# Moving the gated product of a convolutional feed-forward network from VectorE to GpSimd

## The chip, the cores and the metric

One Trainium2 chip, one core of it in use. The metric is the device time of one execution in microseconds (us); lower is better. The engines in the text are PE (TensorE), ACT (ScalarE), DVE (VectorE), POOL (GpSimd) and SP (SyncE, which only issues transfers here).

## What is computed

A decoder trunk of two layers on 576 tokens (512 prompt positions and 8 sequences of 8 new positions) with 1024 features. Each layer is a mixer with three branches followed by a feed-forward network, both with a layer norm behind them. The part that matters here, cut from the reference:

```python
def conv_ffn(h, prefix, w_up, conv_w, conv_b, w_down):
    a = h @ w_up                                   # 1024 -> 2 x 2816
    ext = concatenate([prefix, a], axis=1)         # two earlier rows
    c = conv_b + conv_w[0] * ext[:, 0:T]
    for k in range(1, 3):
        c = c + conv_w[k] * ext[:, k:k + T]
    gate, up = split(c, 2, axis=-1)
    return (silu(gate) * up) @ w_down
```

The change touches the product `silu(gate) * up`, which is the input of the down projection.

## The kernel before

Everything is feature-major: a tile is 128 features by 576 tokens, and the matmuls take 288 tokens at a time. Each fp32 operand of a matmul is split in two parts, hi (fp32r, made by ACT, `weight_hi` and the `copy` at L542) and lo (the remainder, made by DVE, `weight_lo` and `lo` at L1399); a product takes three matmuls (hi times hi, weight hi times input lo, weight lo times input hi), all of them at L981.

The feed-forward network of a layer runs in two halves (`hf`) of 11 feature tiles (`FH`), so there are 44 **pairs** in the program. A pair `j` is a gate tile (par 0) and an up tile (par 1), each one a tile of PE with 8 x 6 matmuls into its own two PSUM banks. In the first half, the first three even pairs (`UP_FIRST = (0, 2, 4)`) are *halved*: tokens 0 to 287 of their tiles were multiplied earlier, beside the layer norm, and parked in `STASH`, so that PE has only 24 matmuls left for each tile. The text calls the other pairs full. After the 11 pairs come the down tiles.

What each engine does for a pair, in its own order:

- PE waits for the weights (`w_lo`) and for its PSUM banks (`mm_free`), and multiplies the two tiles.
- ACT (`up_tile`, L914 to L936), for par 0: wait for PE, copy the prefix and the PSUM banks to `EB` (this frees the banks), split the next weight (hi), wait for `c_ready`, Silu of the gate into `SL`. For par 1: the copies and the weight. Then it waits for `h_ready` and copies `HX` to `HH` (L936), and only then goes on to the next pair.
- DVE (`up_tile`, L1899 to L1943), for each par: three taps of the convolution (L1911, L1918, L1924) and two small copies to `TAIL`; par 0 ends with a drain that releases `c_ready`. The lo part of the weights for pair j+1: in a halved pair both stand within the convolutions, in a full pair the first stands behind par 0 and the second behind the product. Then the product: a drain, a wait for `silu`, two multiplications `SL * CC[1]` into `HX` (L1932 with 512 tokens, L1933 with the 64 sample tokens). Last, a wait for `h_hi` and the lo part of `HX` into `HL` (L1941, shown as L1399).
- POOL has nothing in this stage but the end of the layer norm before it: `norm(l, 2 * l, M_OUT)` ends with 16 additions of a bias (L488). Its next work is `norm(l, 2 * l + 1, M_DOWN[1])`, which begins with the last down tiles.
- SP fetches the weights, one tile ahead.

The first six pairs of the first half are written out, the rest run in loops (`Fori`) on ACT, DVE and PE; the last pair of each half stands behind its loop. The order across engines is set by counting semaphores: `n0`, the number of the pair, is the value that each of them is compared with.

```python
dve.drain()
dve.wait_ge(S["silu"], n0 + 1)
dve.tensor_tensor(HX[:, 0:SEQ], SL[:, 0:SEQ], CC[:, 1, 0:SEQ], ALU.mult)
dve.tensor_tensor(HX[:, SEQ:T]..., seqs(SL[:, CVP:CV], CVS)[:, :, 0:DS], ..., ALU.mult)\
    .then_inc(S["h_ready"], 1)
```

## Time and profile before

| what | value |
|---|---|
| median of 3 runs | 2149.49 us (2149.4 to 2158.35) |
| the profiled execution: its own time | 2150.36 us |
| its span | 2148.5 us |
| PE busy in the span | 2061.5 us, 96% |
| DVE busy | 1199.8 us, 56% |
| ACT busy | 800.5 us, 37% |
| POOL busy | 404.9 us, 19% |
| mean granted clock of PE | 0.986 of full speed |

Read it as a kernel in which PE is busy nearly all of the time, while the other engines feed it. All times of rows are counted from the start of the span. Layer 0 has its first up pairs from 651 us and its second half of pairs from about 848 us; layer 1 has the first up pairs from 1716 us.

### The profile page before, as it was taken

The page shows a single profiled execution, that of the slowest core. Times are in us where ns is not written, and L with a number is a line of the kernel's source. Part 1 is how long each engine was busy: PE and PEld are TensorE (multiplying, and loading weights), DVE is VectorE, ACT ScalarE, POOL GpSimd, SP SyncE. Part 2 cuts the span into 40 slices and gives each one's busy share as a digit, 9 for nine tenths or more (in the row PEclk, how much of TensorE's full clock was granted, in tenths as well). Part 3 has the DMA queues.
Part 4 walks back from the last instruction along what each step waited for, and adds up shares of the span by engine and source line. Part 5 has one row for each costly group of instructions (what it writes and reads, how often), then busy time and mean ns, then how long its engine had stood idle before and what let it go on. Part 6 is the DMA issues. An engine that isn't in the chain of part 4 may idle for free.

```text
span 2148.5 us, 42999 instructions
## 1 busy us (share of the span) xinstructions
PE 2061.5 (96%) x17374; PEld 1903.9 (89%) x17374; DVE 1199.8 (56%) x2036; ACT 800.5 (37%) x1502; POOL 404.9 (19%) x407
## 2 busy tenths in 40 slices
PE   8989999999998999999999899999999999999997
PEld 7976667999998999999989766679999889999997
DVE  4755445333578652666757554453335876436665
ACT  4333445222354331333443343342223543213334
POOL 0025662000051000000350266600001600000012
PEclk9989999999999999999999899999999999999999
DMA  7347996222433232225451499952225332222252
GB/s 259 107 147 283 367 366 248 77 87 79 154 108 98 81 103 66 79 87 175 137 198 64 137 354 364 362 191 88 78 84 167 95 103 78 98 64 87 78 192 72
DMA packets 88849, 325.68 MB, mean 152 GB/s; under 512 B 10576, under 2 KB 15568, under 8 KB 88592
## 3 DMA queue, kind: packets, MB, share of 16 engines
q1 hardware_dynamic: 46512, 169.51, 24.2%
q0 software_dynamic: 37440, 144.98, 18.1%
q10 hardware_dynamic: 4768, 9.37, 1.3%
q8 instruction: 92, 1.51, 0.3%
q14 instruction: 37, 0.30, 0.0%
HBM read 315.52 MB, written 7.26 MB: 150 GB/s over the span
## 4 chain that ended last, share of the span: by engine, by line
PE 84%; DVE 8%; ACT 3%; DMA 2%; issue 1%; DVEq 1%; POOL 0%; ACTq 0%; SPq 0%; POOLq 0%
PE PS L981 64%; PE PS L1229 5%; PE PS L1258 5%; DVE m_WL L1399 2%; PE PS L1249 2%; DMA m_WS<-in_w_units 1%; PE PS L1240 1%; ACT m_WH L542 1%; PE PS L1012 1%; DVE m_X L1433 1%; DVE m_XS L1444 1%; PE PS L1281 1%; DMA m_RAW<-in_cache_wide,m_IDXS 1%; PE PS L1297 1%; PE PS L1288 1%
## 5 line engine op out<-in xcount | busy, mean ns | idle before, releaser
L981 PE MATMUL PS<-m_XS,m_WH 128*128 128x288 f32 x5120 | 922.0, 297 | 30.6 <-DVE m_WL L1399 18.1
L981 PEld LDWEIGHTS PS<-m_XS,m_WH 128*128 128x128 f32 x5120 | 767.1, 189 | 40.0 <-DVE m_WL L1399 21.3
L981 PE MATMUL PS<-m_XS,m_WL 128*128 128x288 f32 x2560 | 583.3, 297 | 0.0
L1399 DVE TENSOR_TENSOR m_WL<-m_WS,m_WH 128x1024 fp32r<-128x1024 f32 (+2 forms) x284 | 369.2, 1302 | 233.1 <-ACT m_WH L542 223.4
L542 ACT ACTIVATE m_WH<-m_WS 128x1024 fp32r<-128x1024 f32 (+2 forms) x284 | 315.2, 1112 | 307.5 <-PE PS L981 287.1
L981 PEld LDWEIGHTS PS<-m_XS,m_WL 128*128 128x128 f32 x2560 | 424.2, 189 | 0.0
L529 POOL DMA_INDIRECT m_RAW<-in_cache_wide,m_IDXS x256 | 242.6, 948 | 397.6 <-PE PS L981 123.0
L472 POOL TENSOR_TENSOR m_XS<-m_X 128x288 f32<-128x288 f32 x8 | 10.6, 1324 | 1182.8 <-DVE m_X L1453 1181.8
L981 PE MATMUL PS<-m_HH,m_WH 128*128 128x288 f32 x704 | 206.8, 300 | 7.7 <-DVE m_WL L1399 7.2
L981 PE MATMUL PS<-m_HL,m_WH 128*128 128x288 f32 x704 | 204.6, 298 | 0.0
L981 PE MATMUL PS<-m_HH,m_WL 128*128 128x288 f32 x704 | 181.4, 299 | 0.0
L981 PEld LDWEIGHTS PS<-m_HH,m_WH 128*128 128x128 f32 x704 | 134.2, 191 | 8.8 <-DVE m_WL L1399 7.7
L981 PEld LDWEIGHTS PS<-m_HL,m_WH 128*128 128x128 f32 x704 | 134.3, 191 | 0.2
L1258 PE MATMUL PS<-m_RAW,m_PT 128*64 128x256 f32 x1024 | 124.6, 385 | 7.3 <-ACT m_PT L542 7.1
L1229 PE MATMUL PS<-m_RAW,m_QSF 64*64 64x256 f32 x1024 | 125.2, 382 | 0.9 <-DMA m_RAW<-in_cache_wide,m_IDXS 0.9
L1229 PE MATMUL PS<-m_RAW,m_QSR 64*64 64x256 f32 x1024 | 124.3, 382 | 0.0
L981 PEld LDWEIGHTS PS<-m_HH,m_WL 128*128 128x128 f32 x704 | 124.2, 190 | 0.0
L1911 DVE TENSOR_SCALAR m_CC<-m_EB,m_PARS 128x592 f32<-128x592 f32 x88 | 51.9, 590 | 127.2 <-ACT m_EB L542 126.7
L1258 PEld LDWEIGHTS PS<-m_RAW,m_PT 128*64 128x64 f32 x1024 | 67.8, 136 | 47.8 <-ACT m_PT L542 14.9
L877 ACT ACTIVATE m_SIG<-PS 128x576 f32<-128x576 f32 x48 | 31.2, 651 | 192.8 <-PE PS L981 192.8
L1742 DVE TENSOR_SCALAR_CACHE_REDUCE PS<-PS,m_NMX 128x512 f32<-128x512 f32 x64 | 48.6, 759 | 90.3 <-PE PS L1240 90.1
L1229 PEld LDWEIGHTS PS<-m_RAW,m_QSF 64*64 64x64 f32 x1024 | 69.1, 132 | 27.1 <-issue 16.2
(274 smaller groups left out, 2900.6 us busy)
## 6 DMA issues: line engine op xcount, KB each, us to landing
m_WS<-in_w_units SPq DMA_DIRECT2D x232, 512.0 KB
m_WS<-in_w_units SPq DMA_DIRECT2D x48, 704.0 KB
m_RAW<-in_cache_wide,m_IDXS POOLq DMA_INDIRECT x256, 6.1
m_X<-in_x_t SPq DMA_DIRECT2D x6, 576.0 KB, 7.2
m_WS<-in_w_units SPq DMA_DIRECT2D x4, 576.0 KB
x_save<-m_X POOLq DMA_DIRECT2D x4, 576.0 KB, 5.2
m_X<-x_save SPq DMA_DIRECT2D x4, 576.0 KB, 7.3
out_y<-m_X SPq DMA_DIRECT2D x8, 288.0 KB, 2.2
```

Of the source, the lines that this page charges most:

```text
L529: pool.indirect_dma_start(raw_of(u)[:, q, :], None, cache_wide.rearrange("l n c -> (l n) c"), bass.IndirectOffsetOnAxis(ap=IDXS[:, l, g:g ...
L542: return nc.scalar.activation(out, in_, ACT.Copy)
L877: nc.scalar.activation(h2(SIG[:, g, :]), pair(g % 2), ACT.Sigmoid)\
L981: mm = pe.matmul(out(half), w(part, k), x(k)[:, half_of(half)], start=(k == 0 and part == 0 and x is xh), stop=(k == last and part == 1))
L1012: mm = pe.matmul(PS[:, bank + h, 0:HT], C["ones"], x[:, h * HT:(h + 1) * HT], start=(k == 0), stop=(k == len(tiles) - 1))
L1229: pe.matmul(PS[64 * c:64 * c + 64, score_bank(u) + h, 0:256], weights, raw_of(u)[rows, c::2, at0:at0 + P], start=(g == 0), stop=False)
L1240: mm = pe.matmul(out[:, :, j, :], QSP[j][rows, rows_of], raw_of(u)[rows, c::2, 2 * KL:ROW], start=False, stop=(j == 1))
L1249: mm = pe.transpose(PS[:, 6, j * P:(j + 1) * P], PRB[:, j * P:(j + 1) * P], ident)
L1258: mm = pe.matmul(PS[64 * c:64 * c + 64, 7, 0:KL], PT[:, a, 64 * c:64 * c + 64], raw_of(u)[:, 2 * (a // 2) + c, j * KL:(j + 1) * KL], start ...
L1399: return dve.tensor_tensor(out, x, hi.bitcast(F32), ALU.subtract)
L1742: dve.tensor_scalar(s0, s0, -SCALE, NMX[:, b, j:j + 1], ALU.mult, ALU.min, accum_out=NMX[:, b, j + 1:j + 2]).then_inc(S["s_max"], 1)
L1911: dve.tensor_scalar(cc, e[:, 2:CV], tap(2), PARS[:, bass.ds(l * NPAR + C_CB + c, 1)], ALU.mult, ALU.add)
```

## The change

The product of all pairs but the last of each half is issued by GpSimd instead of VectorE. VectorE's drain behind the second convolution now counts a new semaphore, `c_pair`. GpSimd waits for it and for `silu`, and multiplies. The two loops of GpSimd stand between its two `norm` calls. The last pair of each half keeps its product on VectorE. ScalarE's program is unchanged: it waits for `h_ready`, whoever counts it. What stood behind the product on VectorE (the weight of par 1, the wait for `h_hi`, the lo part) stays in its order.

```diff
@@ the queue of gpsimd
+            def gated(l, hf, j):
+                n0 = (l * 2 + hf) * FH + j
+                pool.wait_ge(S["c_pair"], n0 + 1)
+                pool.wait_ge(S["silu"], n0 + 1)
+                pool.tensor_tensor(HX[:, 0:SEQ], SL[:, 0:SEQ], CC[:, 1, 0:SEQ], ALU.mult)
+                pool.tensor_tensor(HX[:, SEQ:T].rearrange("p (b t) -> p b t", b=DB),
+                                  seqs(SL[:, CVP:CV], CVS)[:, :, 0:DS],
+                                  seqs(CC[:, 1, CVP:CV], CVS)[:, :, 0:DS], ALU.mult)\
+                    .then_inc(S["h_ready"], 1)
...
                 norm(l, 2 * l, M_OUT)
+                for hf in range(2):
+                    with pool.Fori(0, FH - 1) as j:
+                        gated(l, hf, j)
                 norm(l, 2 * l + 1, M_DOWN[1])
@@ the queue of vector, up_tile
-                def up_tile(hf, j, width, halved=False, last=False):
+                def up_tile(hf, j, width, halved=False, last=False, on_pool=True):
...
-                    dve.drain()
-                    dve.wait_ge(S["silu"], n0 + 1)
-                    dve.tensor_tensor(HX[:, 0:SEQ], SL[:, 0:SEQ], CC[:, 1, 0:SEQ], ALU.mult)
-                    dve.tensor_tensor(HX[:, SEQ:T]..., ALU.mult).then_inc(S["h_ready"], 1)
+                    dve.drain().then_inc(S["c_pair"], 1)
+                    if not on_pool:
+                        dve.wait_ge(S["silu"], n0 + 1)
+                        dve.tensor_tensor(HX[:, 0:SEQ], SL[:, 0:SEQ], CC[:, 1, 0:SEQ], ALU.mult)
+                        dve.tensor_tensor(HX[:, SEQ:T]..., ALU.mult).then_inc(S["h_ready"], 1)
                     if not halved and not last:
                         weight_lo_in_loop(u0 + 3, 1, width)
                     dve.wait_ge(S["h_hi"], n0 + 1)
...
-                    up_tile(hf, FH - 1, UW, last=hf == 1)
+                    up_tile(hf, FH - 1, UW, last=hf == 1, on_pool=False)
```

## Rows read from the trace of the kernel before

**Rows 1.** The page: busy time by engine, and the chain that ended last.
```profile
PE 2061.5 (96%) x17374; PEld 1903.9 (89%) x17374; DVE 1199.8 (56%) x2036; ACT 800.5 (37%) x1502; POOL 404.9 (19%) x407
...
PE 84%; DVE 8%; ACT 3%; DMA 2%; issue 1%; DVEq 1%; POOL 0%; ACTq 0%; SPq 0%; POOLq 0%
```

**Rows 2.** Timeline of PE: start, duration, instruction, idle time before it and releaser.
```profile
668.65 0.53 PE L981 MATMUL PS<-m_XS,m_WH 128*128 128x288 f32 x2 [0.74 <-DVE m_WL L1399]
673.56 0.53 PE L981 MATMUL PS<-m_XS,m_WH 128*128 128x288 f32 x2 [1.45 <-DVE m_WL L1399]
695.31 0.68 PE L981 MATMUL PS<-m_XS,m_WH 128*128 128x288 f32 x2 [2.06 <-DVE m_WL L1399]
...
1760.43 0.82 PE L981 MATMUL PS<-m_XS,m_WH 128*128 128x288 f32 x2 [2.41 <-DVE m_WL L1399]
```

**Rows 3.** Stretches of 3 us: busy PE, PEld, DVE, ACT, POOL, then granted clock.
```profile
693.00:696.00 3.00, 0.94 (x5) 0.70 (x5) 2.91 (x6) 1.84 (x6) 0.00 (x0) 0.92 0.01 3
696.00:699.00 3.00, 3.00 (x14) 3.00 (x14) 2.82 (x6) 0.58 (x1) 0.00 (x0) 0.51 0.58 175
```

**Rows 4.** Timeline, end of pair 0 (halved): the last tap, and ACT's HH.
```profile
661.38 0.83 DVE L1924 SCALAR_TENSOR_TENSOR m_CC<-m_EB,m_PARS,m_CC 128x592 f32<-128x592 f32 x1
...
663.17 0.69 ACT L542 ACTIVATE m_HH<-m_HX 128x576 fp32r<-128x576 f32 x1 [3.95 <-DVE m_HX L1933]
```

**Rows 5.** Timeline of DVE and ACT, pair 1 (full) into pair 2.
```profile
671.54 0.69 DVE L1932 TENSOR_TENSOR m_HX<-m_SL,m_CC 128x512 f32<-128x512 f32 x1
672.15 0.22 DVE L1933 TENSOR_TENSOR m_HX<-m_SL,m_CC 128x64 f32<-128x64 f32 x1
672.28 1.22 DVE L1399 TENSOR_TENSOR m_WL<-m_WS,m_WH 128x1024 fp32r<-128x1024 f32 x1
...
674.09 0.58 DVE L1911 TENSOR_SCALAR m_CC<-m_EB,m_PARS 128x592 f32<-128x592 f32 x1
...
673.43 0.45 ACT L542 ACTIVATE m_EB<-PS 128x224 f32<-128x224 f32 x2
```

**Rows 6.** Timeline, pairs 3 and 5: where ACT waited for PE, and the weight for pair 6.
```profile
689.70 0.22 ACT L542 ACTIVATE m_EB<-m_SFT 128x16 f32<-128x16 f32 x1 [0.56 <-PE PS L981]
710.71 1.23 DVE L1399 TENSOR_TENSOR m_WL<-m_WS,m_WH 128x1024 fp32r<-128x1024 f32 x1
712.98 0.22 ACT L542 ACTIVATE m_EB<-m_SFT 128x16 f32<-128x16 f32 x1 [1.62 <-PE PS L981]
```

**Rows 7.** Timeline of DVE and ACT, pairs 7 to 8 in the loop.
```profile
741.57 0.83 DVE L1924 SCALAR_TENSOR_TENSOR m_CC<-m_EB,m_PARS,m_CC 128x592 f32<-128x592 f32 x1 [0.17 <-issue]
743.45 0.69 ACT L542 ACTIVATE m_HH<-m_HX 128x576 f32 x1 [3.13 <-DVE m_HX L1933]
745.07 0.22 ACT L542 ACTIVATE m_EB<-m_SFT 128x16 f32 x1 [0.93 <-PE PS L981]
746.08 0.59 DVE L1911 TENSOR_SCALAR m_CC<-m_EB,m_PARS 128x592 f32<-128x592 f32 x1 [0.95 <-ACT m_EB L542]
749.08 1.23 DVE L1399 TENSOR_TENSOR m_WL<-m_WS,m_WH 128x1024 fp32r<-128x1024 f32 x1 [0.23 <-issue]
751.47 0.22 ACT L542 ACTIVATE m_EB<-m_SFT 128x16 f32 x1 [1.84 <-PE PS L981]
```

**Rows 8.** POOL: its sum instructions (min/median/max ns), and the end of its bias additions.
```profile
L472 POOL TENSOR_TENSOR m_XS<-m_XS,m_X x44: 800/812/2138, 581.0 to 2128.4; 128x288 f32<-128x288 f32 x44
633.42 20.97 POOL L488 TENSOR_SCALAR m_X<-m_X,m_PARS 128x288 f32<-128x288 f32 x16 [0.22 <-issue]
```

**Rows 9.** Timeline: sums of POOL beside weight splits of DVE.
```profile
1007.78 1.62 DVE L1399 TENSOR_TENSOR m_WL<-m_WS,m_WH 128x1408 fp32r<-128x1408 f32 x1
1008.02 2.06 POOL L472 TENSOR_TENSOR m_XS<-m_X 128x288 f32<-128x288 f32 x1 [353.63 <-DVE m_X L1453]
...
599.48 3.42 POOL L480 TENSOR_TENSOR m_SS<-m_SS,m_LS 128x288 f32<-128x288 f32 x3 [0.79 <-ACT m_LS L568]
602.32 1.67 DVE L1399 TENSOR_TENSOR m_WL<-m_WS,m_WH 128x1024 fp32r<-128x1024 f32 x1
```

More of the change, by code:

```diff
@@ L308, in build @@
                 "xr_hi xr_lo y_hi y_lo m_sum m_hi m_lo",
-                "sf_in e_prefix0 e_prefix1 e_free0 e_free1 c_ready silu h_ready h_hi h_lo",
+                "sf_in e_prefix0 e_prefix1 e_free0 e_free1 c_ready c_pair silu h_ready h_hi h_lo",
         ):
@@ L1929, in up_tile @@
                                 weight_lo_in_loop(u0 + 2, 0, width)
-                    dve.drain()
-                    dve.wait_ge(S["silu"], n0 + 1)
-                    dve.tensor_tensor(HX[:, 0:SEQ], SL[:, 0:SEQ], CC[:, 1, 0:SEQ], ALU.mult)
-                    dve.tensor_tensor(HX[:, SEQ:T].rearrange("p (b t) -> p b t", b=DB),
-                                      seqs(SL[:, CVP:CV], CVS)[:, :, 0:DS],
-                                      seqs(CC[:, 1, CVP:CV], CVS)[:, :, 0:DS], ALU.mult)\
-                        .then_inc(S["h_ready"], 1)
+                    dve.drain().then_inc(S["c_pair"], 1)
+                    if not on_pool:
+                        dve.wait_ge(S["silu"], n0 + 1)
+                        dve.tensor_tensor(HX[:, 0:SEQ], SL[:, 0:SEQ], CC[:, 1, 0:SEQ], ALU.mult)
+                        dve.tensor_tensor(HX[:, SEQ:T].rearrange("p (b t) -> p b t", b=DB),
+                                          seqs(SL[:, CVP:CV], CVS)[:, :, 0:DS],
+                                          seqs(CC[:, 1, CVP:CV], CVS)[:, :, 0:DS], ALU.mult)\
+                            .then_inc(S["h_ready"], 1)
                     if not halved and not last:
```

## The prediction

> **What bounds the kernel.** Read the busy times first: PE is busy for 96% of the span, and the chain that ended last runs through it for 84% [rows 1]. Work taken from DVE therefore gives nothing where PE has its input in time. It can give or cost time only where PE waits, so the timeline of PE in the up stage comes next. In layer 0 it shows three waits worth counting, 0.74, 1.45 and 2.06 us, all for the lo part of a weight [rows 2]; layer 1 repeats the three (its longest, 2.41 us, is shown). They lie at pairs 2 and 4. A halved pair gives PE only 24 matmuls per tile while DVE has the same three taps, two weight splits, product and lo part as for a full pair. Up to pair 5 DVE and ACT, passing work to each other, are as slow as PE or slower. After that PE leads again. The stretches around the longest wait show a second price: the granted clock falls from 0.92 to 0.51, close to the lower of its two levels (1.2 of 2.4 GHz), after PE stood idle, and is full again behind 699 us [rows 3]. About 3 us at half speed cost some 1.5 us.
>
> So three questions decide: how long GpSimd takes for the product, how that moves the first six pairs, and whether the loop pairs, where PE leads, have the slack to hide it.
>
> **The product now.** The last tap of pair 0 ends at 662.21 and ACT starts its copy `HH` at 663.17: 0.96 us from tap to copy [rows 4]. In it are the two multiplications, 0.69 and 0.22 us as durations [rows 5]. Call t the end of the last tap; now `HH` starts at t + 0.96.
>
> **The product on GpSimd, alone.** The trace has no GpSimd multiplication, but 44 sums of two SBUF tiles with 288 elements, 0.80 us at the least [rows 8]. Bounds: if the 0.80 were all fixed, both instructions would take 1.60; if all per element, 576 elements take 1.60 as well. Between the two the result depends on the split. With 0.14 fixed (0.80 less the 0.66 below) and 2.3 ns per element, 512 elements take 1.31 and 64 take 0.29: 1.60 again. A gain over 0.91 is excluded by the first instruction, which cannot be shorter than 0.80 with more elements and still leaves the second. I take 1.60, plus 0.25 to start (two waits in a loop; DVE loses 0.17 to register work before a tap [rows 7]) and 0.08 to wake ACT: `HH` starts at t + 1.93 in a halved pair, 0.97 later than now. The start could be 0.1 or 0.5.
>
> What row and page make of it: DVE's 0.69 and 0.22 and GpSimd's 0.80 are from this trace. The Trainium skill (GPSIMD Engine Reference, section Performance versus the Vector engine) has GpSimd's two-input add 1.96 times as long as VectorE's at 2048 elements; by that ratio the pair of multiplications would be an estimated 1.78 us, and each `HH` 0.2 later still. The case's own row decides, since it has the smaller sizes.
>
> **The product beside a weight split.** In a full pair the change lets DVE start the split for par 1 straight behind the drain, in the same moment that GpSimd is released. The rows show that the two don't run side by side: DVE's split ran from 1007.78 to 1009.40, GpSimd's sum began at 1008.02 and took 2.06 us, to 1010.08, which is 0.68 behind the end of the split; the other way round a split took 1.67 instead of 1.22 behind a sum of GpSimd [rows 5, 9]. So I take it that one of them stands still while the other runs. DVE has one wait fewer and should be first: split from t + 0.13 to t + 1.35, then 0.66 for the first 288 elements, 224 x 2.3 ns = 0.51, 0.29 for the small one, 0.08 to ACT: `HH` at t + 2.89, or 1.93 later than now. If GpSimd gets in first, its large product ends near t + 1.6, the split near t + 2.8 and the small product behind it near t + 3.0: nearly the same for `HH`. Ends: 0.9 later (both products get in before the split) and 2.5 later (a late start on top).
>
> **First six pairs, layer 0** (unrolled; delay of DVE at the start of each pair):
> - Pair 0 is halved: pair 1 starts 0.97 later.
> - Pair 1 is full: + 1.93, less 0.15 that is slack now (the last PSUM copy ends at 673.88, DVE starts at 674.09 [rows 5]): 2.75.
> - Pair 2: + 0.97 = 3.72.
> - Pair 3: ACT now waits 0.56 for PE before its second tile [rows 6], and that is used up: - 0.6 + 1.93 - 0.15 = 4.9.
> - Pair 4: + 0.97 = 5.9.
>
> The weight for pair 6 is ready at 711.94 now, 5.9 later at 717.8. PE wants it at 712.9, when it has done pair 5 [rows 6]. PE loses 4.9 us there, and since it leads from there on it does not get them back. In between the weight for par 1 comes 0.7 earlier relative to its pair, which makes single waits of PE smaller, but pair 6 starts when the chain of DVE and ACT lets it. One thing speaks for less: some of the waits move, and the half clock at 696 us may go or come again elsewhere (1.5 us either way). I count 4.7 for a layer, 9.4 for both. Bounds: with t + 1.5 and t + 1.9 about 1.5 per layer, with the late values about 8.
>
> **The loop pairs.** There are 14 hand-overs in a layer whose earlier pair is GpSimd's and where PE leads (pairs 6 to 9 of the first half, 0 to 9 of the second), 28 in all. Now: t = 742.40, `HH` at 743.45, the prefix of the next pair at 745.07 after 0.93 idle for PE, first tap 1.01 later, weight split 749.08 to 750.31; PE moves on at 751.4 [rows 7]. So there are 1.1 us of slack at the weight and 0.93 at ACT. With `HH` at t + 2.97 (DVE's split starts later in a loop, 0.23 behind the tap) it starts at 745.37. ACT can take the next prefix 0.6 later, or 1.0 if the loop's jump is not hidden, 745.97 to 746.4, and the split ends 0.9 to 1.3 later, 751.2 to 751.6: against 751.4 that is nothing to 0.25 us. I take 0.12 x 28 = 3.3 us. Bounds: 0, and 0.6 each or 17 us if `HH` is another 0.4 later.
>
> **Edits priced at nothing.** The two loops on GpSimd stand in front of its next `norm`, which begins long after the last product; the `norm` in front of them ends at 654.4 [rows 8], 7.8 us before the first product is due, and that margin is the cover. GpSimd issues no transfer in the stage. The count on DVE's drain is no new instruction. The last pair of each half is as before. GpSimd overwrites `HX` only after DVE's count for the next pair, which stands behind DVE's last read of it, so that order asks for no further wait. Behind the product queue ACT's copy and, behind that, ACT's and DVE's next pair.
>
> **Sum.** 9.4 + 3.3 = 12.7 on the profiled execution's 2150.36 (span 2148.5 and 1.86 around it), which is 0.87 above the median: 2149.49 + 12.7 = 2162.2, taken as 2162.
>
> **Rivals.**
> - *The loops become bound by the hand-over.* The slack is nearly used up by my own sum, so 0.4 us more on each product (slow start, a dearer strided 64-element product) makes PE wait 0.52 at each of 28, 14.6, and costs 0.4 at each of five products per layer before that, 4: 9.4 + 4 + 14.6 = 28, so 2177. For it: the narrow margin. Against: 0.80 us is a steady row. Chance 0.22.
> - *Mostly hidden.* Both products get in before the split, or start at once, and the half clock behind the 2.06 wait goes: 1.5 to 4 per layer and nothing in the loops, 2155. For it: 0.08 us is all that other engines need to wake. Chance 0.27.
> - *Faster.* DVE loses 0.91 us per pair, the split for par 1 is ready 0.7 earlier, two waits per layer shrink by 0.7 and the half clock goes: 2.9 per layer, 2143.7. It decides only if `HH` starts before about t + 1.2, since every later one delays the next pair. The 0.80 us of the first instruction alone, with the second behind it, speaks against. Chance 0.03.
> - *The change does nothing*, because ACT had slack for it everywhere: excluded for the first pairs, where DVE starts the next pair within 0.2 us of ACT's copy [rows 5].
>
> Forecast: chance 0.48. The Trainium skill (SBUF — State Buffer, on the shared port pair) gives the pair to whichever starts first for the whole instruction. By that rule the splits at pairs 1 and 3 would end 0.6 later than now where GpSimd is first; the trace has both orders [rows 9], and `HH`, which my sum hangs on, comes out alike in both.
>
> **Numbers.** 0.5% is 10.7 us, about what a measurement of this kernel tells from no change; the border is 2160.2. The forecast's own range is 2157 to 2169, and some 0.3 of its 0.48 lies above the border. With the bound loops, 0.22, and a little of the hidden case: slower 0.56, same 0.41, faster 0.03. The range 2153 to 2178 leaves out the faster case and the outer ends of the two others, under 0.2 together.
>
> **What would show it.** In the changed profile GpSimd's large product should take about 1.3 us in halved pairs and 2.4 in full ones (spanning the split), and ACT's wait for `HX` should grow by 1 and 1.9 us. PE's waits for weights before 720 us should sum to about 9 us instead of 4.3 and stay near nothing from there to 850 us. It would be wrong if the products are under 1 us, if the split isn't a barrier, or if PE waits in every loop pair.

## The result and the profile after

The changed kernel takes 2160.99 us (median of 20 runs, 2156.13 to 2164.86). The kernel before took 2149.44 beside it (20 runs). The ratio is 1.0050, 95% interval 1.0041 to 1.0058: slower by 10.7 us by the ratio, which the text goes by, while the two medians differ by 11.6. The profiled execution took 2159.99 us, its span is 2158.2 and its mean granted clock 0.988. In the code after, PE's matmuls are at L994, ACT's copies at L555, the splits and lo parts of DVE at L1412, the last tap at L1937 and GpSimd's two products at L514 and L515.

The lines of the page that answer to [rows 1]:

```profile
PE 2058.7 (95%) x17374; PEld 1894.2 (88%) x17374; DVE 1200.9 (56%) x1956; ACT 796.4 (37%) x1502; POOL 492.6 (23%) x487
...
PE 80%; DVE 9%; issue 4%; ACT 4%; DMA 2%; DVEq 1%; POOL 1%; ACTq 0%; POOLq 0%; SPq 0%
```

GpSimd's two products in the view of the tile `HX` (min/median/max ns, first and last start):

```profile
L514 POOL TENSOR_TENSOR m_HX<-m_SL,m_CC x40: 1089/1093/1098, 664.1 to 2055.9; 128x512 f32<-128x512 f32 x40
L515 POOL TENSOR_TENSOR m_HX<-m_SL,m_CC x40: 307/1287/1292, 665.2 to 2057.0; 128x64 f32<-128x64 f32 x40
```

DVE has 80 instructions fewer, yet is busy for 1.1 us *more*. The 80 products took 36.5 us (40 x 0.91), and its 1024-wide weight splits now take 316.0 us in all where they took 286.2: most of what DVE no longer computes it spends standing still inside its splits, and the profile counts that as busy. The large product takes 1.09 us in each of the 40 pairs; the small one, with 64 elements, takes 0.31 at the least and 1.29 at the median.

PE's timeline, layer 0, first six pairs, answering to [rows 2]:

```profile
653.35 0.54 PE L994 MATMUL PS<-m_XS,m_WH 128*128 128x288 f32 x2 [0.47 <-DVE m_WL L1412]
670.97 0.53 PE L994 MATMUL PS<-m_XS,m_WH 128*128 128x288 f32 x2 [1.28 <-DVE m_WL L1412]
676.07 0.54 PE L994 MATMUL PS<-m_XS,m_WH 128*128 128x288 f32 x2 [1.64 <-DVE m_WL L1412]
679.96 0.41 PE L994 MATMUL PS<-m_XS,m_WH 128*128 128x288 f32 x1 [0.42 <-DVE m_WL L1412]
...
717.44 0.79 PE L994 MATMUL PS<-m_XS,m_WH 128*128 128x288 f32 x4 [1.54 <-DVE m_WL L1412]
```

The first line starts the second tile of pair 0, the last one pair 6. Between them stand the three waits of pair 2 and three of the same size at pair 4 (1.26, 1.65, 0.42). With the 1.54 at the end they sum to 8.2 us, against 4.25 before. From the second tile of pair 0 to pair 6 PE now takes 717.44 - 653.35 = 64.09 us. In the kernel before the same stretch took 712.92 - 651.59 = 61.33. That is + 2.76 (layer 1: 64.50 against 61.65, + 2.85), less than the waits grew by, because the stretch at half clock of [rows 3] is gone: three windows over the place where it was now show a clock of 1.00.

```profile
693.00:696.00 3.00, 1.84 (x14) 1.84 (x15) 2.69 (x5) 2.18 (x5) 0.00 (x0) 1.00 0.23 38
696.00:699.00 3.00, 1.62 (x13) 1.38 (x11) 2.79 (x2) 0.00 (x0) 1.97 (x2) 1.00 0.35 137
699.00:702.00 3.00, 2.73 (x20) 2.74 (x21) 1.77 (x5) 2.43 (x6) 0.38 (x1) 1.00 0.50 156
```

The hand-over of a halved pair and of a full one, on POOL, DVE and ACT, answering to [rows 4, 5]:

```profile
663.14 0.83 DVE L1937 SCALAR_TENSOR_TENSOR m_CC<-m_EB,m_PARS,m_CC 128x592 f32<-128x592 f32 x1
672.88 0.83 DVE L1937 SCALAR_TENSOR_TENSOR m_CC<-m_EB,m_PARS,m_CC 128x592 f32<-128x592 f32 x1
673.85 2.17 DVE L1412 TENSOR_TENSOR m_WL<-m_WS,m_WH 128x1024 fp32r<-128x1024 f32 x1
...
664.10 1.09 POOL L514 TENSOR_TENSOR m_HX<-m_SL,m_CC 128x512 f32<-128x512 f32 x1 [7.96 <-DVEq L1943]
665.15 0.31 POOL L515 TENSOR_TENSOR m_HX<-m_SL,m_CC 128x64 f32<-128x64 f32 x1
673.84 1.09 POOL L514 TENSOR_TENSOR m_HX<-m_SL,m_CC 128x512 f32<-128x512 f32 x1 [8.38 <-DVEq L1943]
674.89 1.29 POOL L515 TENSOR_TENSOR m_HX<-m_SL,m_CC 128x64 f32<-128x64 f32 x1
...
665.50 0.69 ACT L555 ACTIVATE m_HH<-m_HX 128x576 fp32r<-128x576 f32 x1 [4.53 <-POOL m_HX L515]
676.22 0.69 ACT L555 ACTIVATE m_HH<-m_HX 128x576 fp32r<-128x576 f32 x1 [4.23 <-POOL m_HX L515]
```

Pair 0: t = 663.97, `HH` at t + 1.53. Pair 1: t = 673.71, `HH` at t + 2.51. Read pair 1 as a relay. The large product and the split start within 0.01 us of each other, but the large product takes its full-speed 1.09 us and the split 2.17, its usual 1.22 and 0.95 of standing still. The small product then stands still until the split is done: 1.29 instead of 0.31. The Trainium skill (SBUF — State Buffer, section SBUF: two separate sides) lets one of the two engines hold the port pair that they share for a whole instruction while the other waits; these durations agree.

A loop pair, the same instructions (DVE, POOL, ACT), answering to [rows 7], with PE's first weight load of the next tile (PEld, the part of PE that loads weights):

```profile
746.47 0.83 DVE L1937 SCALAR_TENSOR_TENSOR m_CC<-m_EB,m_PARS,m_CC 128x592 f32<-128x592 f32 x1 [0.17 <-issue]
747.52 2.08 DVE L1412 TENSOR_TENSOR m_WL<-m_WS,m_WH 128x1024 fp32r<-128x1024 f32 x1 [0.21 <-issue]
747.43 1.09 POOL L514 TENSOR_TENSOR m_HX<-m_SL,m_CC 128x512 f32<-128x512 f32 x1 [10.61 <-DVEq L1943]
749.89 0.68 ACT L555 ACTIVATE m_HH<-m_HX 128x576 f32 x1 [4.67 <-POOL m_HX L515]
...
749.66 0.57 PEld L994 LDWEIGHTS PS<-m_XS,m_WH 128*128 128x128 f32 x4 [0.26 <-DVE m_WL L1412]
...
1940.25 0.80 PE L994 MATMUL PS<-m_XS,m_WH 128*128 128x288 f32 x4 [0.28 <-DVE m_WL L1412]
```

t = 747.30. `HH` starts at t + 2.59 (t + 1.05 before) and the split of the next pair's second tile ends at t + 2.30 (t + 2.06 before: 1.22 us from 743.24, t = 742.40). From `HH` to `HH` a pair of the second half took 12.86 us before and takes 12.97 in layer 0, 12.90 and 13.10 in layer 1 (means of nine). The last row is the one wait over 0.25 us that PE's matmul rows show in these 28 pairs, for just that split. The matmul rows hide the rest, because the end of a matmul is modelled. In the rows of PEld 25 of the 28 pairs have a wait, of 0.23 to 0.52 us, 7.3 us in all, and each ends some 0.05 us behind the end of the second tile's split. The kernel before has one such wait, of 0.28.

The waits sum to more than the periods grew, because PE does not go at one pace. Here are two successive runs of matmuls with the high part of the weight, six matmuls from start to start, in the kernel before and in the changed one:

```profile
743.09 0.70 PE L981 MATMUL PS<-m_XS,m_WH 128*128 128x288 f32 x4
743.89 0.70 PE L981 MATMUL PS<-m_XS,m_WH 128*128 128x288 f32 x4
...
747.10 0.69 PE L994 MATMUL PS<-m_XS,m_WH 128*128 128x288 f32 x4
747.89 0.69 PE L994 MATMUL PS<-m_XS,m_WH 128*128 128x288 f32 x4
```

In the kernel before six matmuls take 0.807 us on average (starts at 743.09, 743.89, 744.70, 745.51), in the changed kernel 0.79 (747.10, 747.89, 748.68). A pair has 16 of these steps: 12.91 us at the one pace and 12.64 at the other, without any wait. The granted clock is 1.00 in both. Both kernels go at either pace in turn, for some us or for tens of us, and why PE changes it is open. So a difference of 0.1 us in a period can be pace and not waiting, and the waits are the firmer sign of what holds PE up.

**Where the 9.6 us between the two profiled executions lie.** By the sums of the `HH` intervals and the later first `HH`, layer 0 is 2.5 us longer up to the end of its second half and layer 1 7.4, together 9.9. Outside these stretches the changed kernel is 1.8 us later at the first of them, before GpSimd has made any product, and gets 2.1 back between the layers; the two nearly cancel. Layer 1's parts are 2.85 for the first six pairs, 14 x 0.20 = 2.8 for the loops and some 1.7 for a half clock that sat inside the first six pairs before and now falls behind the 1.75 us wait for pair 6 (granted clock 0.59 at 1783 to 1786 and 0.84 in the 3 us behind). Layer 0's are 2.76 and 14 x 0.11 = 1.5; it came out 1.8 below them. Of that 1.6 lie between the last up tile of the first half and the first one of the second, mostly down tiles: 777.17 to 854.79, 77.62 us, before and 782.18 to 858.21, 76.03 us, now. No matmul row there shows a wait in either kernel. It is the pace again, 2% of 78 us; in layer 1 that stretch takes 77.63 us in the changed kernel too.

### The profile page after: what moved, and what is told of

The parts are those of the page before. It is cut to its first block, busy times and chain, and to the rows that moved or that the text cites. A ratio compares the mean times of both kernels' runs of the same rounds, so it can differ in the third digit from the quotient of the medians.

```text
span 2158.2 us, 43163 instructions
## 1 busy us (share of the span) xinstructions
PE 2058.7 (95%) x17374; PEld 1894.2 (88%) x17374; DVE 1200.9 (56%) x1956; ACT 796.4 (37%) x1502; POOL 492.6 (23%) x487
## 4 chain that ended last, share of the span: by engine, by line
PE 80%; DVE 9%; issue 4%; ACT 4%; DMA 2%; DVEq 1%; POOL 1%; ACTq 0%; POOLq 0%; SPq 0%
PE PS L994 59%; PE PS L1242 5%; PE PS L1271 5%; DVE m_WL L1412 3%; PE PS L1262 2%; PE PS L1253 1%; DMA m_WS<-in_w_units 1%; ACT m_WH L555 1%; DVE m_X L1446 1%; PE PS L1025 1%; PE PS L1294 1%; DVE m_XS L1457 1%; DVE m_CC L1937 1%; PE PS L1310 1%; ACT m_EB L555 1%
## 5 line engine op out<-in xcount | busy, mean ns | idle before, releaser
L994 PE MATMUL PS<-m_XS,m_WH 128*128 128x288 f32 x5120 | 919.3, 297 | 42.2 <-DVE m_WL L1412 26.8
L994 PEld LDWEIGHTS PS<-m_XS,m_WH 128*128 128x128 f32 x5120 | 761.5, 189 | 58.9 <-DVE m_WL L1412 36.2
L994 PE MATMUL PS<-m_XS,m_WL 128*128 128x288 f32 x2560 | 580.8, 296 | 0.0
L1412 DVE TENSOR_TENSOR m_WL<-m_WS,m_WH 128x1024 fp32r<-128x1024 f32 (+2 forms) x284 | 399.0, 1407 | 237.5 <-ACT m_WH L555 221.3
L555 ACT ACTIVATE m_WH<-m_WS 128x1024 fp32r<-128x1024 f32 (+2 forms) x284 | 315.0, 1112 | 306.5 <-PE PS L994 282.5
L994 PEld LDWEIGHTS PS<-m_XS,m_WL 128*128 128x128 f32 x2560 | 422.3, 189 | 0.0
L994 PE MATMUL PS<-m_HH,m_WH 128*128 128x288 f32 x704 | 205.1, 298 | 7.8 <-DVE m_WL L1412 7.3
L994 PE MATMUL PS<-m_HL,m_WH 128*128 128x288 f32 x704 | 203.5, 297 | 0.0
L994 PE MATMUL PS<-m_HH,m_WL 128*128 128x288 f32 x704 | 180.6, 297 | 0.0
L514 POOL TENSOR_TENSOR m_HX<-m_SL,m_CC 128x512 f32<-128x512 f32 x40 | 43.7, 1093 | 580.5 <-DVEq L1943 580.5
L994 PEld LDWEIGHTS PS<-m_HH,m_WH 128*128 128x128 f32 x704 | 133.5, 190 | 8.9 <-DVE m_WL L1412 7.8
L994 PEld LDWEIGHTS PS<-m_HL,m_WH 128*128 128x128 f32 x704 | 133.7, 190 | 0.2
L994 PEld LDWEIGHTS PS<-m_HH,m_WL 128*128 128x128 f32 x704 | 123.8, 190 | 0.0
L555 ACT ACTIVATE m_HH<-m_HX 128x576 f32 (+1 forms) x44 | 30.2, 686 | 195.3 <-POOL m_HX L515 185.6
```

What stands on the lines that cost most here:

```text
L514: pool.tensor_tensor(HX[:, 0:SEQ], SL[:, 0:SEQ], CC[:, 1, 0:SEQ], ALU.mult)
L555: return nc.scalar.activation(out, in_, ACT.Copy)
L994: mm = pe.matmul(out(half), w(part, k), x(k)[:, half_of(half)], start=(k == 0 and part == 0 and x is xh), stop=(k == last and part == 1))
L1412: return dve.tensor_tensor(out, x, hi.bitcast(F32), ALU.subtract)
```

## The experiments

Two theories are told apart. **H**, the prediction's: what costs is `HH`, which comes later; in the first six pairs through the chain of DVE and ACT, in the loops by using up the slack. **S**, formed on the first four runs: in the loops it is the end of the second tile's weight split (below, the split), and `HH` has slack.

The recorded expectations of the first four runs call H "Theory 1"; they take the whole change as 11.5 us, by the medians, and in `loops_only` "34 of the 44 pairs" should be 32, which less the last of each half gives the 28.

Unless said, the edits are to the changed kernel. Differences in us are the ratio less one, times the time of the kernel before. On the chips of the first four and of the last four runs the kernel before takes 2343.52 us (23 runs) and 2329.61 us (35 runs): for these runs the difference to that counts. The extra time lies in another stage, which reads the cache pages: in `first_six_only` PE waits there 109.7 us for ACT's tile `PT`, in the first profile of the kernel before 7.1; why was not looked into. In the middle four runs the kernel before took 2149.08 (29 runs). It was profiled on the first chip alone, and there is one trace of each kernel.

**One part at a time.** `loops_only` keeps the products of the first six pairs on DVE, `first_six_only` those of the loops.

```diff
 loops_only
-                    with pool.Fori(0, FH - 1) as j:
+                    with pool.Fori(0 if hf else 2 * len(UP_FIRST), FH - 1) as j:
-                        up_tile(hf, j, D, halved=j in UP_FIRST)
+                        up_tile(hf, j, D, halved=j in UP_FIRST, on_pool=False)
```

> GpSimd makes the product in the loop pairs alone (34 of the 44 pairs before, less the last of each half: 28 hand-overs), VectorE in the first six pairs of each layer. Theory 1 (the cost is the late hand-over, in both places): PE goes from its first up tile at pair 0 to pair 6 in 61.3 to 61.7 us as in the kernel before (64.1 and 64.5 in the changed one), the loops keep the changed kernel's period of 12.94 to 13.17 us between two copies HH (12.80 to 12.93 before), and the time is 4 to 6 us over before, about 2154.5. Theory 2 (as the prediction split it: the first six pairs carry nearly all): 0 to 3 us over before, period as before.

Measured: ratio 1.0024 (1.0012 to 1.0035), + 5.6 us. `HH` period in the second halves 12.96.

```diff
 first_six_only
-                for hf in range(2):
-                    with pool.Fori(0, FH - 1) as j:
-                        gated(l, hf, j)
+                with pool.Fori(0, 2 * len(UP_FIRST)) as j:
+                    gated(l, 0, j)
...
-                        up_tile(hf, j, D)
+                        up_tile(hf, j, D, on_pool=False)
```

> GpSimd makes the product in the first six pairs of each layer, VectorE in all loop pairs. Theory 1: pair 0 to pair 6 takes 64.1 to 64.5 us as in the changed kernel, the loops are back at 12.80 to 12.93 us, the time is 5 to 7 us over before, about 2155. Theory 2: 8 to 10 us over before, about 2158.5. Together with the run of the loops alone the two differences should add up to the 11.5 us of the whole change under either theory; if they add up to clearly less, the two places interact.

Measured: 1.0022 (1.0008 to 1.0037), + 5.2 us. Period 12.89, the first six as in the changed kernel. The two add up to the whole, 10.8 of 10.7, though each is known to some 3 us only. So each part costs about half. The trace of `loops_only` itself shows only 28 x 0.08 = 2.3 us in its periods (the interval of its time begins at 2.8), and 6.0 us in 21 waits at the second tile's split.

**The split behind the product.** DVE waits for the product before it starts the split, so nothing of GpSimd's stands still, and `HH` comes a microsecond *earlier*.

```diff
                     if not halved and not last:
+                        if on_pool:
+                            dve.wait_ge(S["h_ready"], n0 + 1)
                         weight_lo_in_loop(u0 + 3, 1, width)
```

> As the changed kernel, but in full pairs VectorE's weight split for par 1 waits until GpSimd has made the product, so the two never run side by side. Theory 1a (the collision is what makes the hand-over late in full pairs): HH starts 1.53 us behind the last tap in every pair (now 2.51 in full ones), the split takes 1.22 instead of 2.17 and the small product 0.31 instead of 1.29; the loops are back near 12.88 us and the time falls by 4 to 7 us, to about 2155. Theory 1b (GpSimd's own slowness is what costs, the collision is covered): the split ends 0.5 later, HL not earlier, the time stays within 2 us of the changed kernel, 2159 to 2163.

Measured: 1.0100 (1.0078 to 1.0122), + 23 us. Neither theory had that. A loop pair, DVE and PE:

```profile
858.70 0.84 DVE L1937 SCALAR_TENSOR_TENSOR m_CC<-m_EB,m_PARS,m_CC 128x592 f32<-128x592 f32 x1 [0.17 <-issue]
861.15 1.23 DVE L1412 TENSOR_TENSOR m_WL<-m_WS,m_WH 128x1024 fp32r<-128x1024 f32 x1 [1.61 <-POOL m_HX L515]
...
862.43 0.81 PE L994 MATMUL PS<-m_XS,m_WH 128*128 128x288 f32 x4 [0.58 <-DVE m_WL L1412]
```

`HH` starts at t + 1.60 (861.14), the split ends at t + 2.84, and the period is 13.51 with a wait of 0.42 to 0.64 us for that split in every pair. It is the observation that made theory S.

**The large product twice**, with a drain between (`HX` is written with the same values again).

```diff
-                pool.tensor_tensor(HX[:, 0:SEQ], SL[:, 0:SEQ], CC[:, 1, 0:SEQ], ALU.mult)
+                for _ in range(2):
+                    pool.tensor_tensor(HX[:, 0:SEQ], SL[:, 0:SEQ], CC[:, 1, 0:SEQ], ALU.mult)
+                    pool.drain()
```

> As the changed kernel, but GpSimd makes the large product (512 tokens) twice, with a drain between, so each HH is 1.1 to 1.2 us later. Theory 1: nothing is left to hide it. Five hand-overs in the first six pairs of each layer give 11 us, the 28 in the loops 31 to 34 us: 42 to 45 us over the changed kernel, about 2204. Theory 2 (the loops hide the product): only the first pairs pay, 11 us, about 2172.

Measured: 1.0153 (1.0131 to 1.0175), + 36 us, between the two expectations. Period 13.37 on average, the split as in the changed kernel, `HH` at t + 3.8:

```profile
867.13 0.84 DVE L1939 SCALAR_TENSOR_TENSOR m_CC<-m_EB,m_PARS,m_CC 128x592 f32<-128x592 f32 x1 [0.17 <-issue]
868.18 2.08 DVE L1414 TENSOR_TENSOR m_WL<-m_WS,m_WH 128x1024 fp32r<-128x1024 f32 x1 [0.22 <-issue]
...
871.80 0.69 ACT L557 ACTIVATE m_HH<-m_HX 128x576 f32 x1 [5.92 <-POOL m_HX L517]
```

So a late `HH` does cost the loops. PE's waits here lie mostly at the weight of the next pair's *first* tile, as H has it: PEld shows 26 of them, 18.4 us, just behind that split, and 6 at the second tile's, 2.7 us.

**S against H.** `split_before_count` has GpSimd in the loops alone and puts the split ahead of the count that releases GpSimd: the split is early and untouched, `HH` later still.

```diff
+                    if on_pool:
+                        weight_lo_in_loop(u0 + 3, 1, width)
                     dve.drain().then_inc(S["c_pair"], 1)
...
-                    if not halved and not last:
+                    if not halved and not last and not on_pool:
                         weight_lo_in_loop(u0 + 3, 1, width)
```

> As loops_only (GpSimd makes the product in the loop pairs alone), but there VectorE makes the weight split for par 1 before it counts c_pair, so the split is never held up and the product comes later: the split ends 1.45 us behind the last tap (2.30 in the changed kernel, 2.06 before), HH starts 3.0 to 3.1 us behind it (2.6 now in a loop, 1.05 before). Theory S (the loops of the changed kernel are set by the split of par 1, which GpSimd's large product holds up by 0.95 us, and not by the late HH): the period between two HH falls from 12.96 back to the 12.87 of the kernel before, the time is within 2 us of before. Theory H (the loops are set by the late HH): the period rises to 13.1 or more, the time is 8 to 14 us over before.

Measured: 2149.11 us, ratio 1.0002 (0.9988 to 1.0016), period 12.80. A pair of its loop:

```profile
875.23 0.84 DVE L1937 SCALAR_TENSOR_TENSOR m_CC<-m_EB,m_PARS,m_CC 128x592 f32<-128x592 f32 x1 [0.17 <-issue]
875.98 1.22 DVE L1412 TENSOR_TENSOR m_WL<-m_WS,m_WH 128x1024 fp32r<-128x1024 f32 x1
...
878.82 0.69 ACT L555 ACTIVATE m_HH<-m_HX 128x576 f32 x1 [4.85 <-POOL m_HX L515]
```

`HH` is at t + 2.75, later than in the changed kernel, and the cost of the loops is gone: 0 with an interval of 3 us either way. H falls as the account of the loops' cost. Not one wait is left at the second tile's split. What the late `HH` does show is 13 waits of 0.18 to 0.36 us, 3.5 in all, just behind the split of the *first* tile, as in this row:

```profile
872.18 0.56 PEld L994 LDWEIGHTS PS<-m_XS,m_WH 128*128 128x128 f32 x4 [0.36 <-issue]
```

So the slack that H counts is just used up here, and PE's faster pace covers these waits. Put side by side, the end of the split and the period are t + 1.13 and 12.80 here, t + 2.06 and 12.88 before, t + 2.30 and 12.97 to 13.10 changed, t + 2.84 and 13.51 above. The first two differ by pace: the kernel before has a single wait at that split, of 0.28 us.

**The small product first**, so that GpSimd gives way to the split after 0.3 us instead of 1.09.

```diff
-                pool.tensor_tensor(HX[:, 0:SEQ], SL[:, 0:SEQ], CC[:, 1, 0:SEQ], ALU.mult)
                 pool.tensor_tensor(HX[:, SEQ:T]..., ALU.mult)
-                    .then_inc(S["h_ready"], 1)
+                pool.tensor_tensor(HX[:, 0:SEQ], SL[:, 0:SEQ], CC[:, 1, 0:SEQ], ALU.mult)\
+                    .then_inc(S["h_ready"], 1)
```

> As the changed kernel, with GpSimd's two products in the other order. One of two instructions with two SBUF inputs stands while the other runs: the small product takes 0.31 us and gets in first, the split is held up by 0.2 to 0.3 only (1.5 instead of 2.17 us), then the large product waits for the split and ends 2.6 to 2.7 us behind the last tap (small product 2.45 now). Theory S: the loops are back at 12.87 us, the first six pairs cost 0.4 us more per layer through HH, and the whole is 3 us under the changed kernel, 8 to 9 over before. Theory H: the loops get 0.1 to 0.2 us per pair slower, 15 to 17 us over before.

Measured: 2155.0 us, ratio 1.0030 (1.0014 to 1.0045), + 6.4 (3.0 to 9.7), nearer to the expectation of S, which its interval holds. Pair 1, DVE and POOL:

```profile
675.51 1.39 DVE L1412 TENSOR_TENSOR m_WL<-m_WS,m_WH 128x1024 fp32r<-128x1024 f32 x1
675.51 0.31 POOL L514 TENSOR_TENSOR m_HX<-m_SL,m_CC 128x64 f32<-128x64 f32 x1 [8.38 <-DVEq L1943]
675.78 2.07 POOL L517 TENSOR_TENSOR m_HX<-m_SL,m_CC 128x512 f32<-128x512 f32 x1
```

The split takes 1.39 instead of 2.17, `HH` stays at t + 2.5, the loops' period is 12.83 with one wait at the second tile's split, of 0.21 us, and the first six pairs take 64.10 us as in the changed kernel. What is left is the six-pair term: S again.

**The chain of the first six pairs.** Here both kernels hang on `HH` of one pair holding up ACT and DVE for the next. `store_later` is the kernel *before* with `HH` and `HL` of pairs 0 to 4 issued within the next pair's taps; `store_later_on_gpsimd` is the same edit to the changed kernel, where DVE also waits for `silu` in place of the store that it puts off.

```diff
+                            if before is not None:
+                                store(before, n0 - 1)
...
-                    act.wait_ge(S["h_ready"], n0 + 1)
-                    copy(HH[:, j, :] ..., HX[:, :]).then_inc(S["h_hi"], 1)
+                    if not leave:
+                        store(j, n0)
```

> The kernel before (all products on VectorE), but in the first six pairs of a layer the copy HH and the lo part HL of pair j are made within pair j+1 (ScalarE behind its copies to EB for par 0, VectorE behind the weight split of par 0), so VectorE starts the next pair without waiting for ScalarE's HH. If the chain tap, product, HH, EB copy, tap is what makes PE wait at pairs 2 and 4 (0.74, 1.45 and 2.06 us), 1.5 us fall away behind each halved pair and PE reaches pair 6 some 3 to 5 us earlier per layer, the half clock near 696 us goes, and the time is 6 to 10 us under before. Rival: VectorE's own work, 19.6 us for a halved and a full pair against 19.2 of PE, leaves only the slack to win, 1 to 2 us per layer, 2 to 4 in all.

Measured: 2151.0 us, ratio 1.0007 (0.9999 to 1.0016). That is outside both expectations. PE takes 61.4 us from pair 0 to the end of pair 5, as before (61.4), but now with two waits in place of three:

```profile
675.84 1.22 DVE L1406 TENSOR_TENSOR m_WL<-m_WS,m_WH 128x1024 fp32r<-128x1024 f32 x1
...
677.12 0.53 PE L988 MATMUL PS<-m_XS,m_WH 128*128 128x288 f32 x2 [2.44 <-DVE m_WL L1406]
698.86 0.54 PE L988 MATMUL PS<-m_XS,m_WH 128*128 128x288 f32 x2 [2.44 <-DVE m_WL L1406]
```

Both wait for the split of a full pair, which stands behind the product, while the next tile, a halved one, keeps PE busy for only some 3.2 us. Freed from the chain, the pairs run into the split's place.

> The same deferral of HH and HL in the first six pairs, on top of the changed kernel. There the late HX no longer stands in the chain of the first six pairs, and VectorE is rid of 0.91 us per pair; against that the split of par 1 is still held up by 0.95. Theory: the first six pairs then cost nothing against before or win 1 to 3 us per layer, and only the loops' cost of the changed kernel stays (4 to 6 us): 0 to 5 us over before. Rival (the chain isn't what costs in the first six pairs): still 9 to 11 us over before.

Measured: 2154.7 us, ratio 1.0032 (1.0018 to 1.0047), + 6.9, between the two expectations, with the same two waits at 2.69 and 2.68, and the loops at 12.93 to 13.07 with 25 waits at the second tile's split, 7.9 us. From pair 0 to the end of pair 5 PE takes 61.7 us in both layers. The changed kernel took 63.3 and 63.7 and waited for pair 6 on top, the kernel before 61.4 and 61.7, `store_later` 61.4 and 61.8. So once no pair waits for `HH` of the pair before, it makes next to no difference in the first six which engine multiplies: their term is the chain through `HH`. What is left is the loops' cost.

**Both edits, and each alone.** `store_later_splits_early` adds to `store_later` the split of full pairs within the convolutions, where halved pairs have it; `splits_early` has that edit alone.

```diff
-                        up_tile(hf, j, D, halved=j in UP_FIRST)
+                        up_tile(hf, j, D, halved=True, before=j - 1 if j else None, leave=j < first - 1)
```

> The kernel before, with its products on VectorE and two edits in the first six pairs of a layer: the HH copy and the HL subtraction of a pair are issued within the next pair's taps, as in store_later, and the split of the second tile of a full pair is placed where that of a halved pair is, within the convolutions, instead of behind the product. Theory P (what was left in store_later, the two gaps of TensorE of 2.44 us, is the position of that split, since the next halved tile keeps TensorE busy for only about 3.2 us): the split is ready before that, both gaps go, and TensorE needs 57 to 58.5 us from its second tile of pair 0 to pair 6 instead of 61.33; 3 to 4 us a layer, 6 to 8 in all, so 2141 to 2143 where the kernel before takes 2149. Rival (VectorE's own sum of work, about 19.6 us for a halved and a full pair against TensorE's 19.2, is the bound, or the late HL subtraction holds the taps up): the gaps come back elsewhere, 0 to 2 us gained.

Measured: ratio 0.9965 (0.9949 to 0.9981), 8.2 us *less* than the kernel before. PE from pair 0 to the end of pair 5: 57.6 us (743.21 to 800.8), with two waits of 1.08 and a granted clock of 1.00 in the windows behind both. It beats both kernels.

> The kernel before with only the split of the second tile of a full pair among the first six placed within the convolutions. HH of the full pairs stays where it is, at 0.96 us behind the last tap, which is itself 1.22 us later. Theory P says that both matter: the two gaps that wait for the split go, and the chain from tap over HH and HL to the next pair becomes 1.2 us longer in each full pair, so TensorE from pair 0 to pair 6 takes 60 to 62.5 us (61.33 before) and the whole is within 2 us of the kernel before. Rival (the split alone set the pace, as in the loops): 57 to 59 us, 5 to 8 us gained in all.

Measured: 1.0038 (1.0017 to 1.0060), + 8.9 us, outside both expectations. PE's waits in layer 0:

```profile
765.13 0.54 PE L981 MATMUL PS<-m_XS,m_WH 128*128 128x288 f32 x2 [1.12 <-DVE m_WL L1399]
771.51 0.80 PE L981 MATMUL PS<-m_XS,m_WH 128*128 128x288 f32 x4 [2.92 <-DVE m_WL L1399]
795.48 0.80 PE L981 MATMUL PS<-m_XS,m_WH 128*128 128x288 f32 x4 [2.92 <-DVE m_WL L1399]
```

The windows from the first 2.92 on (the granted clock is the third number from the right):

```profile
771.00:774.00 3.00, 2.49 (x14) 2.49 (x15) 2.12 (x4) 0.72 (x3) 0.00 (x0) 0.80 0.43 117
774.00:777.00 3.00, 3.00 (x16) 3.00 (x16) 1.92 (x4) 1.72 (x5) 0.00 (x0) 0.63 0.14 57
```

The chain through `HH` became 1.2 longer per full pair, as expected. What was not expected is the clock behind each long wait: 3 x 0.20 + 3 x 0.37 = 1.7 us lost, twice a layer. With it PE takes about 65.5 us (744.47 to ACT's copy of its last tile at 809.99), 4.1 more than before, and two layers make 8.2. One edit alone loses 8.9 us, the other changes nothing that can be told, both together win 8.2.

**The changed kernel with the split ahead of the count everywhere.** The edit to DVE's queue of `split_before_count`, with GpSimd in the first six pairs too.

```diff
+                    if on_pool and not halved:
+                        weight_lo_in_loop(u0 + 3, 1, width)
                     dve.drain().then_inc(S["c_pair"], 1)
...
-                    if not halved and not last:
+                    if not halved and not last and not on_pool:
                         weight_lo_in_loop(u0 + 3, 1, width)
```

> The changed kernel, products on GpSimd in all pairs but the last of each loop, with the second tile's split put ahead of the count that releases GpSimd in all full pairs, the first six among them. Theory S (in the loops the end of that split is what the next pair waits for; in the first six it is the chain over HH): the loops' period falls back to 12.8 to 12.87 us although HH comes at 2.7 us behind the last tap, and the six-pair term of 2.8 us a layer stays: 5 to 7 us over the kernel before. Theory H (late HH costs the loops too): the loops at 13.0 or more and 11 us or more over the kernel before.

Measured: 1.0037 (1.0021 to 1.0054), + 8.6 us; period 12.85, pair 0 to pair 6 at 64.6 us in either layer. One wait is left at the second tile's split in the loops, of 0.36 us, and the six-pair term stays, slightly grown. The time alone does not decide: its interval, 4.9 to 12.6 us, holds the 5 to 7 of S and the 11 of H. The period does, which H had at 13.0 or more.

**GpSimd with everything in its favour**: `store_later_splits_early` with the products on GpSimd, and the split ahead of the count in the loops.

```diff
                     dve.drain().then_inc(S["c_pair"], 1)
...
-                    dve.wait_ge(S["h_hi"], n0 + 1)
+                    if leave:
+                        if on_pool:
+                            dve.wait_ge(S["silu"], n0 + 1)
+                    else:
+                        store(j, n0)
```

> GpSimd multiplies as in the changed kernel, with everything that the runs so far point to: the HH copy and HL subtraction deferred into the next pair in the first six, the second tile's split within the convolutions there and ahead of the count in the loops. It differs from store_later_splits_early by the engine of the products alone. If freeing VectorE of 0.91 us a pair is worth anything once nothing waits for the product, it is 2 to 5 us faster than store_later_splits_early; if VectorE's time was not the bound, within 2 us of it; if GpSimd's product collides with the next pair's taps (each of which it would hold up by up to 1 us), 2 to 6 us slower.

Measured: 0.9958 (0.9940 to 0.9976), 9.8 us less than the kernel before, within 2 us of `store_later_splits_early`. The expectation says that the two differ by the engine of the products alone; this one also has the split ahead of the count in the loops. One of its first six pairs, DVE's next tap and the two products:

```profile
768.84 1.30 DVE L1936 TENSOR_SCALAR m_CC<-m_EB,m_PARS 128x592 f32<-128x592 f32 x1 [0.24 <-issue]
...
768.73 1.09 POOL L514 TENSOR_TENSOR m_HX<-m_SL,m_CC 128x512 f32<-128x512 f32 x1 [8.91 <-DVEq L1959]
769.77 0.53 POOL L515 TENSOR_TENSOR m_HX<-m_SL,m_CC 128x64 f32<-128x64 f32 x1
```

The next pair's first tap stands still behind the large product, 1.30 instead of 0.59. Ten first taps are held up like that. The 0.91 us a pair that DVE is spared come back there in part as 0.5 to 0.7 of standing still. The two kernels can't be told apart: each of the two differences, 9.8 and 8.2 us, is known to some 4 us.

## Why the prediction came out as it did

The time lay inside the forecast's own range, 1 us below its 2162, and the mechanism named for the first six pairs is the one that the runs show. That the sum came so close is in part luck: the first six pairs were priced 3.8 us too high, the loops 1.0 (by period) to 2.3 us (by `loops_only`) too low and for the wrong reason, and the 1.7 us of half clock in layer 1, which the prediction allowed for without a price, came on top.

- **The product alone.** Forecast 1.31 and 0.29 us; measured 1.09 and 0.31. The sums of [rows 8] were taken as 0.14 and 2.3 ns per element. From 0.80 at 288 elements to 1.09 at 512 it is 1.3, and from 0.31 at 64 to the 0.80 it is 2.2: no one line holds them. The whole is 1.40 and not 1.60, and the start took 0.13 instead of 0.25: `HH` at t + 1.53 instead of t + 1.93.
- **Beside the split.** The barrier is as described. Which engine gets in first was wrong: I gave it to DVE, and GpSimd had it in all 34 full pairs. So the large product does not span the split in a full pair, 1.09 us and not the 2.4 that was to show it; the small one does. As the prediction said, `HH` hardly depends on that (t + 2.51 instead of 2.89). But the split does: it ends at t + 2.3 where I had t + 1.35, and I closed that point with `HH`, "which my sum hangs on".
- **First six pairs.** The chain with the measured values, + 0.57 and + 1.55 in place of 0.97 and 1.93: 0.57, then 1.97, 2.54, 3.34 and 3.91 at pair 5, less the 0.96 that PE had in hand at pair 6, is 2.95. Measured 2.76 and 2.85. The step was right and its term, 4.7 a layer, mis-sized by its two inputs: 5.6 in place of 9.4. PE's waits came to 8.2 us, against the 9 of the prediction. The half clock went in layer 0, one of the two ways allowed for it; in layer 1 it only moved, some 1.7 us.
- **Loops.** This step failed in its reason. It had the late `HH` use up the slack of ACT and the weight of the *first* tile, 0 to 0.25 us. `split_before_count` has a later `HH` and costs nothing. What costs is the weight of the *second* tile, which the prediction had becoming ready 0.7 us earlier; it came 0.24 later, held up behind the large product. By period it cost 14 x 0.11 + 14 x 0.20 = 4.3 us, by `loops_only` 5.6 (2.8 to 8.2), in place of 3.3. The prediction's own sign against itself, that PE waits in every loop pair, nearly came true: 25 of 28, by the rows of PEld.
- **Rivals.** The loops bound by the hand-over (2177) is a real mechanism. With `HH` at t + 3.8 (`large_product_twice`) the period is 0.49 us longer than before, about the 0.52 a pair that the rival gave to t + 3.37; nothing between t + 2.75 and t + 3.8 was run. Mostly hidden (2155) asked for `HH` without the split's time in it; that did not happen. Faster did not happen, and `best_on_gpsimd` speaks against it in general: with nothing waiting for the product, freeing DVE of it gained 1.6 us, in a difference known to some 6.

The six-pair cost is shown by `first_six_only`. That its mechanism is the chain through `HH` is shown from two sides: `small_product_first` frees the split and not `HH` and leaves the stretch at 64.10, and `store_later_on_gpsimd` frees the next pair from `HH` and brings the stretch back to that of `store_later`. Open is what sets PE's pace, and with it how the loops' 7.3 us of waits become 4 to 6 of time. Not tried was a kernel in which GpSimd shares nothing with DVE.

## What to carry to other kernels

Moving work from a busy engine to an idle one pays only if something waits for the busy engine's *time*; here others waited for its *results*, and the slower engine delivers them later. When two engines can't run side by side, price the instruction that is held up, and ask who waits for that one, and not just for the product that was moved. Look for short waits in the rows of the weight loads too: the matmul rows showed a single wait over 0.25 us in the loops, these showed 25. Where two waits close on each other (here `HH` of the last pair and the weight of the next), removing one alone can win nothing or lose, and both together win: test the pair before giving up on either.

## What the runs showed of the hardware that I had not expected

- Released by the same drain, GpSimd got its instruction in before DVE's own next one in all 34 full pairs of the changed kernel: by 0.01 us in the six that are written out (673.84 against 673.85), by 0.08 to 0.10 in the loops (747.43 against 747.52). The large product never took over 1.098 us in 40 pairs, so it never stood behind a split.
- A 64-element product that takes 0.31 us alone took 1.29 behind a split and 0.53 behind a tap.
- A PE wait of 2.92 us cost 1.7 more through the clock, while waits of 1.28, 1.64 and 0.42 within 10 us cost nothing; in layer 1 a wait of 1.75 us did. In `store_later` the first wait of 2.44 left the clock at 1.00 and the second, in the same layer, was followed by windows at 0.78 and 0.65. In layer 1 it was the other way round, the first (2.45) brought the clock down (0.79 and 0.64) and the second (2.81) did not. So the length of a wait does not decide it here. A change that splits one long wait into several short ones can still come out cheaper than the sum of its waits says, as in layer 0 of the changed kernel.
- With the granted clock at 1.00 PE's matmuls of 288 columns came six to 0.79 us in some stretches and six to 0.807 in others, 0.27 us a pair apart. No run here tells what switches between the two.
